# One address remainder for the operands of the expert products, and the down bias as a full product

## The reference

```python
logits = h @ router_w + router_b
top_vals, top_idx = top_k(logits, 4)           # 4 of 32 experts for each token
gates = softmax(top_vals)
# for each expert e, on the tokens x that chose it:
gu = x @ w_gu[e] + b_gu[e]                     # (n, 1024) @ (1024, 2048)
gate, up = split(gu)
gate, up = minimum(gate, 7), clip(up, -7, 7)
act = (up + 1) * gate * sigmoid(1.702 * gate)
y = act @ w_down[e] + b_down[e]                # (n, 1024) @ (1024, 1024)
# out[token] += gates * y
```

## The kernel before, in words

| tile | before | remainder | after | remainder |
|---|---|---|---|---|
| e_hi | 162976 | 160 | same | 160 |
| e_lo0, e_lo1 | 195744, 203936 | 160 | same | 160 |
| e_lo2, e_lo3 | 82048, 90240 | 128 | 82080, 90272 | 160 |
| x_hi, x_lo | 212128, 216224 | 160 | same | 160 |
| act_hi, act_lo | 104576, 108672 | 128 | 104608, 108704 | 160 |
| bias_d, ones_b | 140416, 141440 | 128 | 140416, 142464 | 128 |

## Time and profile before

### The profile page before, as it was taken

The page is one execution under the profiler, slowest core; times in us unless marked ns, Lnnn a source line. Parts: engine busy times, 40 slices in busy tenths (PEclk is TensorE's granted clock), DMA queues, the critical chain, the costliest instruction groups (busy, mean ns, idle before and its releaser), DMA issues.

```text
span 1568.9 us, 21558 instructions
## 1 busy us (share of the span) xinstructions
PE 1485.3 (95%) x7059; PEld 1155.6 (74%) x7060; DVE 1247.9 (80%) x1119; ACT 1073.7 (68%) x1136; POOL 318.1 (20%) x262
## 2 busy tenths in 40 slices
PE   3999997999899999999999999999999999999993
PEld 1657874457688888888888888888888888888872
DVE  1476757156798899999999998999999999998992
ACT  4442347254788887777777888887777777888881
POOL 1000000301032222222222222222222222322221
PEclk9999998998899999999999999999999999999996
DMA  9555530245799999999999999999999999999964
GB/s 330 174 168 212 212 104 1 73 183 193 282 365 363 359 351 365 361 368 361 359 365 368 368 375 364 352 363 364 360 369 360 354 363 373 373 367 359 349 264 124
DMA packets 97663, 475.17 MB, mean 303 GB/s; under 512 B 26320, under 2 KB 36536, under 8 KB 45408
## 3 DMA queue, kind: packets, MB, share of 16 engines
q1 hardware_dynamic: 85120, 451.45, 74.9%
q0 software_dynamic: 12512, 23.31, 5.6%
HBM read 468.62 MB, written 23.67 MB: 314 GB/s over the span
## 4 chain that ended last, share of the span: by engine, by line
PE 91%; ACT 3%; DVE 2%; DMA 2%; issue 1%; SPq 1%; POOLq 0%; DVEq 0%; ACTq 0%; POOL 0%
PE bank L1460 15%; PE bank L1461 15%; PE bank L1462 15%; PE bank L1483 8%; PE bank L1484 7%; PE bank L1485 7%; PE bank L1307 4%; PE bank L1118 3%; PE bank L1119 3%; PE bank L1120 3%; PE bank L1441 2%; PE bank L1433 2%; PE bank L1075 1%; PE bank L1268 1%; PE bank L1454 1%
## 5 line engine op out<-in xcount | busy, mean ns | idle before, releaser
L1590 DVE TENSOR_TENSOR e_lo<-ring,e_hi 128x2048 fp32r<-128x2048 f32 x384 | 868.2, 2289 | 88.4 <-ACT e_hi L759 88.3
L759 ACT ACTIVATE e_hi<-ring 128x2048 fp32r<-128x2048 f32 x384 | 730.4, 1920 | 236.2 <-PE bank L1462 230.5
L1460 PE MATMUL bank<-e_hi,x_hi 128*128 128x512 f32 x1024 | 405.7, 396 | 2.7 <-DVE e_lo L1590 2.7
L1461 PE MATMUL bank<-e_lo,x_hi 128*128 128x512 f32 x1024 | 405.1, 396 | 0.0
L1462 PE MATMUL bank<-e_hi,x_lo 128*128 128x512 f32 x1024 | 403.3, 394 | 0.0
L1460 PEld LDWEIGHTS bank<-e_hi,x_hi 128*128 128x128 f32 x1024 | 193.5, 189 | 53.8 <-issue 7.2
L1462 PEld LDWEIGHTS bank<-e_hi,x_lo 128*128 128x128 f32 x1024 | 193.2, 189 | 42.0
L1461 PEld LDWEIGHTS bank<-e_lo,x_hi 128*128 128x128 f32 x1024 | 193.4, 189 | 41.3
L1483 PE MATMUL bank<-e_hi,act_hi 128*128 128x512 f32 x512 | 206.1, 403 | 0.5 <-DVE act_lo L1603 0.5
L1484 PE MATMUL bank<-e_lo,act_hi 128*128 128x512 f32 x512 | 202.5, 395 | 0.0
L1485 PE MATMUL bank<-e_hi,act_lo 128*128 128x512 f32 x512 | 202.2, 395 | 0.0
(11 more groups left out here) (237 smaller groups left out, 1547.6 us busy)
## 6 DMA issues: line engine op xcount, KB each, us to landing
ring<-in_w_gu SPq DMA_DIRECT2D x256, 1024.0 KB, 7.9
ring<-in_w_down SPq DMA_DIRECT2D x128, 1024.0 KB, 7.1
ring<-in_ada_w SPq DMA_DIRECT2D x24, 1024.0 KB, 9.0
ring<-in_w_in SPq DMA_DIRECT2D x9, 1024.0 KB, 7.0
ring<-in_w_o SPq DMA_DIRECT2D x4, 1024.0 KB, 6.5
ring<-in_w_in SPq DMA_DIRECT2D x10, 256.0 KB, 6.1
xs<-in_x SPq DMA_DIRECT2D x4, 512.0 KB, 5.3
xn_rows<-area POOLq DMA_DIRECT2D x4, 512.0 KB, 3.6
```

What stands on the lines that cost most here:

```text
L759: return nc.scalar.activation(dst, src, ACT.Copy, scale=scale)
L1460: pe.matmul(bank[b][:], x_hi[:, c, :], hi, start=False, stop=False)
L1461: pe.matmul(bank[b][:], x_hi[:, c, :], lo, start=False, stop=False)
L1590: tt(e_lo[c % PARTS][:], raw(period.raw_slot(c)), e_hi[:, c % PARTS, :].bitcast(F32), ALU.subtract).then_inc(lo_ready, 1)
```

## The change

The two tail places of `e_lo` and the two tiles `act_hi` and `act_lo` move up by 32 bytes (`tail_at`), so that all operands of the expert products leave 160 modulo 512. The down bias no longer uses two row groups: all 1024 values of a bias row (in three bf16 rows) lie side by side in partitions 0 to 2, the other 125 partitions hold zeros, and each of the two products takes all 128 rows. The zeros are written once, by GpSimd. The bias tile becomes 1024 bytes longer, and `ones_b` moves behind it.

```diff
-        bias_g, bias_d = view(14336, 256).bitcast(BF16), view(14592, 256).bitcast(BF16)
-        ones_b = view(14848, P // 2).bitcast(BF16)
+        bias_g, bias_d = view(14336, 256).bitcast(BF16), view(14592, 512).bitcast(BF16)
+        ones_b = view(15104, P // 2).bitcast(BF16)
...
-        e_lo_at = [nc.sbuf_base, nc.sbuf_base + 4 * SLOT, area_at, area_at + 4 * SLOT]
+        tail_at = area_at + (nc.sbuf_base - area_at) % 512
+        e_lo_at = [nc.sbuf_base, nc.sbuf_base + 4 * SLOT, tail_at, tail_at + 4 * SLOT]
...
-        act_hi = nc.alloc_sbuf_tensor_at("act_hi", [P, KD, P], F32R, offset=area_at + 4 * 5632)
-        act_lo = nc.alloc_sbuf_tensor_at("act_lo", [P, KD, P], F32R, offset=area_at + 4 * 6656)
+        act_hi = nc.alloc_sbuf_tensor_at("act_hi", [P, KD, P], F32R, offset=tail_at + 4 * 5632)
+        act_lo = nc.alloc_sbuf_tensor_at("act_lo", [P, KD, P], F32R, offset=tail_at + 4 * 6656)
...
             def down_bias(e):
-                for g in range(2):
-                    for h in range(2):
-                        sp.dma_start(bias_d[32 * g:32 * g + 3, 256 * h:256 * h + 256],
-                                     bias_d_dram[2 * g + h, e, :, :]).then_inc(d_rows_in, 16)
+                for g in range(4):
+                    sp.dma_start(bias_d[0:3, 256 * g:256 * g + 256], bias_d_dram[g, e, :, :]).then_inc(d_rows_in, 16)
...
             done(nc.gpsimd.memset(ones_b, 1.0))
+            done(nc.gpsimd.memset(bias_d, 0.0))
...
                 for q in range(2):
-                    rows = slice(32 * q, 32 * q + 3)
-                    pe.matmul(bank[4 + q][:], ones_b[rows, :], bias_d[rows, :], start=True, stop=False)
+                    pe.matmul(bank[4 + q][:], ones_b, bias_d[:, q * 512:q * 512 + 512], start=True, stop=False)
```

## The result

| | median us | runs | ratio to before, 95% interval |
|---|---|---|---|
| before | 1571.74 | 4 | |
| changed kernel | 1552.37 (1551.51 to 1553.23) | 4 | 0.9879 [0.9862, 0.9897] |

A forecast was written before the change was run, and what follows sets the result against it. TensorE's steps between product starts were taken to bound the expert loop. Gate-up 6.5 us plus down 11.2 us gave 17.7 us saved, 1553.3 from the profiled execution or 1554.3 from the median; stated 1553.5 us, range 1549.5 to 1561.

The forecast's parts named there:

- gate-up chunks 1 to 7: Gate-up products behind the first chunk: equal remainders bring every chunk to 2.72 us, saving 0.21 us an expert.
- down chunks 1 to 3: Down products behind the first chunk: with all operands at remainder 160, they save 0.20 us an expert.
- run-up with the bias products: From last transpose to second down product: two full bf16 bias products cut 0.86 us to 0.78, saving 0.08.
- rest of down chunk 0: Eleven products behind the first down step: 2.56 us becomes 2.49 with equal remainders and no row-group switch, saving 0.07.
- x 32: Summing step: the down savings of 0.20 + 0.08 + 0.07 us count for all 32 experts, 11.2 us.
- rival of the low part of memory: Place, not remainder, makes e_lo's tail and act slow; only the bias edit gains 2.9 us, to 1569.2; chance 0.05.
- counter-test: Down chunks: e_lo's tail places cost 0.05 us a gate-up chunk but nothing where act is at 128 (2.78 against 2.81).
- no address could matter: Prediction's reading of the skill's independent TensorE read ports: the address term would be 0, leaving only the bias edit.
- rival that the full pair keeps all switching costs: Down bias: serial 128-row pair takes 1.08 us against 0.86; slower overall 0.02, 1566 with the addresses' gain 0.04.
- The trail is seen only behind row groups: First chunks: a disturbance of some 0.06 us outlasts the first step only behind row groups, so the full 0.07 was taken.
- The first down product followed after 0.23 and not 0.34: Sign in the profile after: the step from first to second down product shrinks from 0.34 us to 0.23.
- So no new wait should take the gain back: Expert loop: VectorE rises only to 92% and weight loads need some 373 GB/s, so neither becomes the bound.

The follow-up runs named there:

- e_lo alone: Changed kernel with act_hi and act_lo back at remainder 128, e_lo's tail places staying at 160: 1560.55 us, 0.9930 of the kernel before.
- address edit alone: Kernel before with only e_lo's tail places and both act tiles moved 32 bytes up, down bias as before: 1555.43 us, 0.9901.
- bias edit alone: Kernel before with only the down bias changed to full 128-row products, addresses as before: 1567.75 us, 0.9978.
- x pads: Changed kernel with a pad moving x_hi and x_lo up: by 32 bytes 1571.23 us, by 128 bytes 1568.06 us, by 256 bytes 1552.31 us.
- serial three-row kernel: Changed kernel with both down-bias products taking only their 3 rows, in the first row group, one after the other: 1564.12 us, 0.9949.
- act alone moved: Changed kernel with e_lo's tail places back at remainder 128, act staying at 160: 1562.61 us, 0.9943 of the kernel before.
- kernel without the stride: Changed kernel with the activation stored as all even, then all odd features, so its transposes read contiguously and VectorE writes strided: 1551.18 us, 0.9863.
- all at 0: Changed kernel with a 352-byte pad ahead of the tiles, putting all operands of the expert products at remainder 0: 1554.78 us, 0.9895.
- tail 64 up: Changed kernel with e_lo's tail places, act_hi and act_lo 64 bytes further up, at remainder 224: 1571.34 us, 1.0000 of the kernel before.

## Why the prediction was right

The predicted 1553.5 us (1549.5 to 1561) against 1552.37. By terms, in us an expert (means over the 29 experts from 440 to 1480 us of each profile, taken from its starts in ns; single rows of 0.01 us give 0.21 for the second term and 0.05 for the fourth):

| term | predicted | measured | shown by |
|---|---|---|---|
| gate-up chunks 1 to 7 | 0.21 | 0.22 | timeline after; e_lo alone gives it too |
| down chunks 1 to 3 | 0.20 | 0.20 | address edit alone |
| run-up with the bias products | 0.08 | 0.09 | bias edit alone |
| rest of down chunk 0 | 0.07 | 0.065 | 0.045 with the address edit alone, none with the bias edit alone |
| one expert | 0.56 | 0.586 | |

The spans fell from 1568.9 to 1551.1, by 17.8 where 17.7 was summed. That this agrees to 0.1 is luck: small errors cancel. The 30 turns between the first gate-up product of the second expert (405.75 before, 405.50 after) and that of the last (1490.24 and 1472.42) gave 17.57, where the sum has 30 x 0.56 = 16.8; ahead of them came 0.25 that the sum does not have. From there to the end both kernels take 78.7 us, so the 0.9 that the sum still has there (one gate-up, two down products) did not come. The first 0.59 of it did, up to the transposes of the last activation (1524.97 before, 1506.56 after). Behind them the down bias of the last expert waits for VectorE, in both kernels:

```profile
1531.64 0.61 PE L1473 MATMUL bank<-area 3*128 3x512 bf16 x2 [5.56 <-DVE area L1849]
```

```profile
1513.96 0.63 PE L1472 MATMUL bank<-area 128*128 128x512 bf16 x1 [6.29 <-DVE area L1848]
```

After, the first product of the pair has no record; its load starts 6.99 us behind those transposes, where it was 6.64 before, so 0.35 go back here. The rest goes back in the last down product, whose first steps behind the wait take 0.43 in both kernels (granted clock 0.51 from 1532 to 1536 us before, 0.50 from 1514.6 to 1518.6 after: the 1.2 GHz level), and in what follows it. The step that was off, in small, is thus "x 32": the terms pay in the loop and not at its end.

The medians fell by 19.4: the profiled execution before lay 0.8 below its median, the one after 0.9 above. The prediction allowed for part of the first; the second is scatter, and the 1.1 us between 1553.5 and 1552.37 lie inside what the measurement can tell (its interval is 2.8 us to either side).

**What bounds.** Right. Inside the loop no step was given back; ScalarE still waits 221.3 us for TensorE to free a part of e_hi, and SP 568.4 + 248.8 us for slots that VectorE frees.

**Equal remainders, and not the place.** The counter-test that the prediction read from the down chunks (2.78 against 2.81) was sound: moving e_lo away from act made these chunks slower, and 32 bytes on x took a chunk from 2.72 to 2.80 with its other operands in place. The rival of the low part of memory is refuted. The rule of the Trainium skill that stood against the term ("SBUF — State Buffer", "Who interferes with whom": two independent ports, TensorE waits for nobody) speaks of engines that wait for engines, and from 430 to 1500 us TensorE does wait for none. What does not hold is the prediction's step from there to "no address could matter": the x pads would then have changed nothing, and the one of 32 bytes cost 19 us.

**The price of row groups.** Right, and isolated by the serial three-row kernel: 1.07 against 0.77. The rival that the full pair keeps all switching costs is refuted by the same pair of numbers. The rule that weight loads overlap only where the row group differs ("TensorE: Matmul & The Clock Gate", "The mechanism") fails here: with the full pair every load, from the last transpose to the second down product, starts while a product of the same rows runs. It is the loads into and out of the row groups that start late (1008.06 and 1008.38 above).

**Where its reasoning failed.** Three places, all small.
- "The trail is seen only behind row groups." The trail is what the rest of a first chunk takes above 11 x 0.2267 = 2.49. It is not seen there alone: with act alone moved, the rest of down chunk 0 takes 2.53 us (1004.65 to 1007.18) behind full products. And with the bias edit alone nothing of the 0.07 came (2.56 as before). The term belongs to the addresses: 2.56 is eleven products at 0.233, with no trail to lose. Only some 0.02 are the bias edit's. What sets the length of the trail, from 2.50 to 2.55 with equal operands, is open. Chunks with the same operands behind the same bias products differ: down chunk 0 takes 2.50 in the changed kernel and 2.53 with x 32 bytes up, gate-up chunk 0 2.55 in the changed kernel and 2.52 with act back at 128. So these operands alone do not set it; whether what ran further ahead does was not tried.
- "The first down product followed after 0.23 and not 0.34" was a bad sign to name: recorded starts show 0.41 there. Only the sum across the bias could be tested. The two bias products 0.22 apart show where both are recorded, with the bias edit alone (a row of 0.59 for products of 0.38). The other signs came as named: 2.72 a chunk, 35.5 an expert, 2.90 for gate-up chunk 0.
- "So no new wait should take the gain back." None did in amount, but the next limit is nearer than was said: in the kernel without the stride TensorE waited once for the gate-up bias rows, which SP had issued 11 us earlier behind five loads of weights.

**The memset and the down-bias transfers** cost nothing that the trace shows (the memset takes 0.96 us): the first gate-up product starts at 369.76 us, and at 369.3 in the kernel with the address edit alone, which has neither; both lie in the scatter of 368.6 to 372.7.

## What to carry to other kernels

For a stream of full fp32r products, give the stationary and the moving operands the same byte remainder modulo 256, as far as the distances below show; a chunk of 12 products costs 3% more without it, and a shift of 32 bytes decides. Read such costs from starts of products in a place where one operand alone changes, and look for a second place where the same tile meets another partner before blaming the tile. A product of few rows is worth its row groups only where enough of them run side by side: leaving and entering cost 0.30 us here, a full 128x512 bf16 product 0.22. For the four products of the gate-up bias that makes full ones dearer, by an estimate from these two numbers (0.77 + 2 x 0.22 = 1.21 for the run-up, against the 0.88 from the last transpose, 1010.28, to the second gate-up product, 1011.16, that it takes now); it was not run. And a saving per turn of a loop is paid only where the same engine still bounds: count the turns, and look at the last one.

## What the runs showed of the hardware that was not expected

At the full granted clock (1.00, the 2.4 GHz level), for fp32r products of 128x512 with a weight load each:

| stationary minus moving, bytes | mean step of a product, us | from |
|---|---|---|
| 0 (both at 160, or both at 0) | 0.2267 | changed kernel, all at 0 |
| +32 | 0.2333 | x 32 up |
| -32 | 0.2333 | act at 128, e at 160 |
| +64 | 0.2333 | tail 64 up, down chunk 1 |
| +128 | 0.2323 | x 128 up, mean of seven chunks |
| +256 | 0.2267 | x 256 up |

At 2.4 GHz these are 544 and 560 clocks. Distances other than these were not run, and why the distance matters is open. The cost is not one of the single product: in the gate-up chunks 2 and 3 before, one product in three had an unequal operand (e_lo), yet a chunk took 2.77, two thirds of the way from 2.72 to 2.80, and its single steps went from 0.226 to 0.235. With all operands equal they are 0.226 or 0.227, once the trail behind a bias product is over. Transposes whose stationary operand has a stride of 8 bytes step at 0.120 us, contiguous ones at 0.109; a VectorE write of 128x1024 fp32 in two interleaved halves takes 2.03 us against 1.22.
